# Experts' loop of a two-block transformer on one core: all twelve low parts of a block's weights on VectorE

## The reference, cut to what matters

```python
for e in range(N_EXPERTS):
    he = jax.nn.silu(h @ w1[e]) * (h @ w3[e])
    out = out + gates[:, e:e + 1] * (he @ w2[e])
```

## Time and profile before

| what | value |
|---|---|
| median of three runs | 2589.7 us |
| the profiled execution | 2601.98 us, of which the span from first to last instruction is 2600.2 us |
| experts' loop in the trace | about 2243 to 2574 us of the span |
| one turn, from the third on | 18.50 us |
| TensorE busy over the span | 2328.2 us (90%) |
| VectorE busy over the span | 1598.8 us (61%) |
| GpSimd busy over the span | 177.3 us (7%) |
| mean granted TensorE clock | 0.941 of full speed |

### The profile page before, as it was taken

How to read it: one execution, slowest core, us unless ns; L and a number is a source line. 1 busy time by engine, 2 the same in 40 slices (tenths; PEclk the granted TensorE clock), 3 DMA queues, 4 the chain that set the end, 5 groups by cost and what they waited for, 6 DMA issues and landing times. The chain is left out here.

```text
span 2600.2 us, 32144 instructions
## 1 busy us (share of the span) xinstructions
PE 2328.2 (90%) x11490; PEld 1867.7 (72%) x11490; DVE 1598.8 (61%) x2267; ACT 1067.3 (41%) x1615; POOL 177.3 (7%) x201
## 2 busy tenths in 40 slices
PE   4998688899999999878979999999997788799995
PEld 3777566678878777757757888788885676577774
DVE  6564656555566555465655555763353765599996
ACT  3443234333351334233344333323313434577774
POOL 0001100000000000101000000000000001122222
PEclk9998899899999899789889999998996999799997
DMA  7640000222235355000012222442365001699995
GB/s 295 221 158 1 1 34 1 81 87 90 97 118 189 104 191 182 20 1 2 33 49 81 97 89 95 165 156 89 107 218 193 1 1 42 267 397 397 396 397 211
DMA packets 95239, 348.20 MB, mean 134 GB/s; under 512 B 12288, under 2 KB 14352, under 8 KB 94864
## 3 DMA queue, kind: packets, MB, share of 16 engines
q1 hardware_dynamic: 88496, 323.57, 35.3%
q0 software_dynamic: 3888, 14.16, 1.4%
q10 hardware_dynamic: 2736, 8.92, 0.8%
HBM read 333.50 MB, written 21.50 MB: 137 GB/s over the span
## 5 line engine op out<-in xcount | busy, mean ns | idle before, releaser
L498 PE MATMUL ps<-a_hi,w_hi 128*128 128x512 f32 x1408 | 571.5, 406 | 42.3 <-DVE y_lo L1775 19.3
L500 PE MATMUL ps<-a_hi,w_lo 128*128 128x512 f32 x1408 | 563.8, 400 | 0.0
L499 PE MATMUL ps<-h_lo,w_hi 128*128 128x512 f32 x1280 | 507.3, 396 | 0.0
L462 DVE TENSOR_TENSOR w_lo<-ring,w_hi 128x1024 fp32r<-128x1024 f32 x178 | 218.1, 1226 | 378.9 <-ACT w_hi L457 378.5
L457 ACT ACTIVATE w_hi<-ring 128x1024 fp32r<-128x1024 f32 x178 | 188.3, 1058 | 534.2 <-PE ps L500 521.0
L498 PEld LDWEIGHTS ps<-a_hi,w_hi 128*128 128x128 f32 x1408 | 268.2, 190 | 114.9 <-DVE w_lo L462 28.5
L500 PEld LDWEIGHTS ps<-a_hi,w_lo 128*128 128x128 f32 x1408 | 267.7, 190 | 66.3
L499 PEld LDWEIGHTS ps<-h_lo,w_hi 128*128 128x128 f32 x1280 | 243.2, 190 | 60.7 <-issue 2.9
L3061 DVE TENSOR_TENSOR moe_w_lo<-p,moe_w_hi 128x1024 fp32r<-128x1024 f32 x187 | 247.0, 1365 | 14.9 <-ACT moe_w_hi L3160 13.6
L3160 ACT ACTIVATE moe_w_hi<-p 128x1024 fp32r<-128x1024 f32 x204 | 216.1, 1062 | 68.8 <-PE ps L3103 61.3
L1998 PE MATMUL ps<-p_lo,down_hi 128*128 128x512 f32 x352 | 137.9, 392 | 0.0
(11 more groups left out here) (619 smaller groups left out, 4295.2 us busy)
## 6 DMA issues: line engine op xcount, KB each, us to landing
ring<-in_ffn_up SPq DMA_DIRECT2D x88, 512.0 KB, 3.4
ring<-in_w_in SPq DMA_DIRECT2D x72, 512.0 KB, 4.6
p<-in_moe_gate SPq DMA_DIRECT2D x68, 512.0 KB, 6.1
p<-in_moe_up SPq DMA_DIRECT2D x68, 512.0 KB, 5.5
p<-in_moe_down SPq DMA_DIRECT2D x68, 512.0 KB, 6.9
vt<-in_ada SPq DMA_DIRECT2D x64, 512.0 KB, 3.9
down_raw<-in_ffn_down SPq DMA_DIRECT2D x32, 704.0 KB, 4.9
y<-in_ada SPq DMA_DIRECT2D x32, 512.0 KB, 3.6
```

What stands on the lines that cost most here:

```text
L462: self.c.nc.vector.tensor_tensor(self.c.w_lo[:, s % 2, :], self.c.slot(s), self.c.w_hi[:, s % 2, :].bitcast(F32), ALU.subtract).then_inc(s ...
L498: nc.tensor.matmul(bank, c.w_hi[:, s % 2, at], hi(kt), start=(kt == 0), stop=False)
L499: nc.tensor.matmul(bank, c.w_hi[:, s % 2, at], lo(kt), start=False, stop=False)
L500: return nc.tensor.matmul(bank, c.w_lo[:, s % 2, at], hi(kt), start=False, stop=(kt == KT - 1))
```

## The change

VectorE makes the low part of chunk 5 too, between those of chunks 4 and 6. GpSimd's subtraction is replaced by an addition of one number per partition (zero plus zero into a spare column), which waits for nothing. Nothing else is touched: loads, ScalarE, TensorE and the semaphores stay, and `low[5]` is now set by VectorE.

```diff
+        self.spare = c.small.bitcast(I32)[:, 56:57]
...
             def body(j):
-                subtract_chunk(pool, nc.gpsimd, 5, j)
+                nc.gpsimd.tensor_tensor(m.spare, m.zero[:, 0:1], m.zero[:, 0:1], ALU.add)
                 choose(j + 2)
                 pool.wait_ge(now, j + 3)
                 nc.gpsimd.tensor_tensor(m.now[:, 1:2], m.zero[:, 0:1], m.zero[:, 0:1], ALU.add)
...
                 if not first(j):
                     lower_he(j - 1)
-                lower(j, (4, 6, 7))
+                lower(j, (4, 5, 6, 7))
                 if not first(j):
                     lower(j - 1, (8, 9, 10, 11))
                 product(j)
```

## The result

The changed kernel takes 2578.3 us in the median of five runs (2575.2 to 2583.2), the kernel before, timed with it, 2590.4. The ratio is 0.9939, interval 0.9920 to 0.9958: 15.8 us by the ratio, 12.1 by the medians, 12.9 by the means of the five and five. The kernel got faster, by about 12 us where 9.6 were forecast.

The account below looks back on a forecast made before the run. It took GpSimd's subtraction, which stalls TensorE and excludes VectorE, to bound the loop. Saving 14 by 0.63, 8.8 us, plus 0.8 at the end, 9.6 us, took 2589.7 to 2580.1 us; range 2577.5 to 2585.5.

Parts of the forecast that it names:

- TensorE's wait for GpSimd: In the loop, TensorE stalls 15 times on chunk 5's low part from GpSimd; 0.63 us a turn would come back.
- VectorE's full turn: In the loop, VectorE's old turn of 18.50 us included 1.59 standing still; it would lose 2.03 and gain 1.17.
- The turn: One loop turn, set by TensorE, would fall from 18.50 to 17.87 us.
- 14 stalls: Stalls of turns 2 to 15 removed, 14 by 0.63 us: 8.8 us saved.
- VectorE's sum: VectorE's new loop turn from pitches, twelve low parts by 1.17 plus other work: 17.64 us, 0.23 under TensorE's.
- The second rival: In the loop, GpSimd's small operations hold VectorE up, up to 0.19 us each; time 2585.3 us; chance 0.08.
- The end: After the loop, VectorE reaches the last block's chunk 10 low part about 0.8 us earlier: 0.8 us saved.
- VectorE's share: At the end, VectorE's earlier arrival at the low part of chunk 10, about 0.8 us.
- Transfers: First rival: in the loop, transfers take over as the bound; 2581 to 2585 us, say 2583; chance 0.12.
- New stall on VectorE: In the loop, TensorE waits for VectorE at chunk 4 or 5; gain gone, about 2589 us; chance 0.07.
- The stretch not GpSimd's: In the loop, VectorE's long low part has another cause and its 1.59 us stay; 2600.7 us; chance 0.04.

Follow-up runs that it names:

- Experiments 3: Changed kernel, but GpSimd subtracts unrelated tiles at its old moment, for nobody, in place of the small addition; ratio 1.0048 to the kernel before, turn 19.54 us.
- Experiment 4: Changed kernel, but GpSimd makes the low part of the previous block's chunk 10, in time, VectorE the other eleven; ratio 0.9989 to the kernel before, turns 18.37 us.
- Experiment 6: Changed kernel plus a GpSimd fill of 128 x 3072 unused numbers with zeros, reading nothing; ratio 0.9965 to the kernel before, turns 17.83 us.
- experiment 5: Changed kernel with VectorE's low parts in order 4, 6, 5, 7, so chunk 5's is late; ratio 1.0050 to the kernel before, turns 18.96 us.
- the other two old ones: Second and third traces of the kernel before, unchanged; from first transposes of gathered rows to the end 359.0 and 359.7 us.
- the repeats: The changed kernel, unedited, timed twice more against the kernel before; ratio 0.9952 both times.
- experiment 2: Changed kernel without GpSimd's small addition; ratio 0.9959 to the kernel before, turns 17.83 us.

## Why the prediction was right in its way and too small

**What bounded the kernel.** Right: VectorE and GpSimd exclude each other. Experiments 3 and 4 show it, with low parts of 3.42 and 2.16 us where 1.21 is the rule. Experiment 6 shows that a GpSimd fill of 2.67 us doesn't do it; that this is because a fill doesn't read SBUF is likely, but no run isolates it. I gave TensorE's wait for GpSimd the leading part and VectorE's full turn a second one. Experiment 4 shows that the freeze alone suffices: with the wait gone and the freeze left, 0.13 of 0.67 us return. And the wait itself came of the exclusion: GpSimd started at 2397.61 and takes 2.41 us alone, so it would have been done at 2400.02, ahead of TensorE's 2400.35 (an estimate from the rows and sums of the prediction).

**The turn.** Forecast 17.87, measured 17.83, with 0.67 us back where the sum had 0.63. Over 14 stalls that is 9.3 and not 8.8 us (from the first transposes to those of turn 15: 295.25 us in the first old trace, 285.96 in the new). The 36 matmuls of the second turn, which I took for TensorE's free pace, still had a little of the rising clock in them: 8.25 us, or 8.21 as I corrected them, where the changed kernel takes 8.17.

**VectorE's sum** was wrong, and by luck on the safe side. The four low parts that gave 1.17 us each have 0.14 us of idle time before the last; back to back one costs 1.135. VectorE's own turn is 17.21 us and not 17.64, its idle time in the changed kernel 0.62 and not 0.23, and the stretch in the old kernel 1.73 (2.948 less 1.216) and not 1.59. The second rival would have needed 0.62 us a turn, not 0.23. The hand-overs came as worked out: chunk 4's low part is ready 0.46 us before TensorE wants it (forecast 0.4), chunk 5's 0.68 (forecast 0.65). An order worse by one subtraction costs 1.13 us a turn (experiment 5).

**The end: the step that was mis-sized.** This term is the step of the sum that failed, more than the 0.5 us of the stalls. The sum had 0.8 us beyond the 14 stalls. Measured were 2.5 between the first two traces, 1.3 to 1.6 against the other two old ones, and 1.9 on the average of three and three (from the transposes of turn 15 to the end: 65.6, 64.4 and 64.4 us before, 63.1, 62.9 and 62.8 after). VectorE's share came out as forecast: the low part of the last block but one's chunk 10 ended 17.12 us earlier in absolute time, of which 7.01 lay ahead of the loop and 9.29 were stalls, which leaves 0.82. "The load, output and final sums follow unchanged" was the wrong sentence: it put at nothing, without a reason, the change in the load's landing. The load after it landed in 5.16, 4.93 and 4.96 us in the traces of the changed kernel (6.08, 5.63 and 5.80 before), 0.8 us sooner on average, as much again as VectorE's share. Why it lands sooner I did not test. Between the first two traces TensorE's last 24 matmuls also took 7.5 and not 8.7 us, since fewer of them ran at the half clock (7 and 12 matmuls of 0.63 us); the other two old traces have 7.5 and 7.4, so this part is chance of the first.

**The time.** Stalls 9.3 and end 1.3 to 2.5 make 10.6 to 11.8 us; the three and three loops differ by 11.0, the three ratios say 12.4 twice and 15.8 once. The forecast of 9.6 was 13 to 23% under these 11.0 to 12.4. On the old median of 2589.7 the repeats give 2577.3, just under the range's 2577.5, and the first ratio 2573.9. So of the 6.2 us between 9.6 and that first 15.8, 0.5 are the stalls and 0.5 to 1.7 the end. The other 4 or 5 lie in no turn and at no end that the traces show, and their cause stays open. Chance is enough to explain them: loop starts scatter by 18 us whichever kernel runs (2225.5 to 2243.0 in the eleven traces of the changed kernel and its variants), and the same five and five runs give 12.1 us by their medians. That the change moves something ahead of the loop is not excluded by three old traces. The range had been drawn for the loop's unknowns and left out this scatter of everything ahead of it; that was its fault.

**The rivals.** *Transfers:* not seen in the time, and nearer than I thought. I judged 397 GB/s not to be the most and was right; the most in this loop is 411 to 412, just what TensorE's turn asks for. At 2% less, by the same arithmetic, the first rival would have eaten into the gain. *Small operations:* nothing (experiment 2). *New stall on VectorE:* none in the turns; TensorE is busy throughout. *The stretch not GpSimd's:* refuted, none of 204 is above 1.227 us.

## What to carry to other kernels

Work given to GpSimd that reads SBUF need not be free for VectorE: here a subtraction of 2.4 us cost VectorE 0.95 to 2.2 us of standing still (low parts of 2.16, 2.95 and 3.42 us) to spare it 1.135. Where it falls counts as much as its length: the 0.95 us fell in a chain with 0.46 to spare and cost 0.54 a turn. When two engines disturb each other and a third waits, test lateness and freezing apart (an unneeded operation at the same place; the same operation where it is in time) before crediting either. Take an engine's own pace from a stretch without any pause: 0.14 us of idle time hidden in four operations made VectorE's floor 0.43 us too high. And ask of every floor under the one that is removed how far down it lies: here TensorE's 17.83 us and the transfers' 17.8 were the same.

## What the runs showed of the hardware that was not expected

A DMA share near 1 said little: it was 1.02 at 397 GB/s with loads landing after 5.9 to 6.7 us, 1.03 at 412 with 7.8 to 8.1, and 1.03 at 411 with 15.8. The landing times told when the transfers had become the bound; the share and the rate did not.

The loop starts between 2226.4 and 2244.3 us after the same code, and between the two traces at the ends of that range it went with the clock. These are the stretches 0:500, 500:1060 and 1060:1400 us of the kernel before in its second trace (loop start 2244.3) and in its third (2226.4), columns as above, the granted clock third from the end:

```profile
0.00:500.00 500.00, 409.13 (x2277) 323.66 (x2278) 295.74 (x532) 185.83 (x366) 25.21 (x46) 0.91 0.28 99
500.00:1060.00 560.00, 540.88 (x2288) 429.63 (x2287) 331.71 (x379) 210.31 (x272) 3.79 (x5) 0.98 0.38 129
1060.00:1400.00 340.00, 288.48 (x1727) 230.03 (x1726) 191.95 (x415) 121.53 (x274) 21.77 (x38) 0.86 0.07 22
```

```profile
0.00:500.00 500.00, 411.80 (x2284) 322.67 (x2285) 295.63 (x532) 185.97 (x366) 25.38 (x46) 0.95 0.28 100
500.00:1060.00 560.00, 540.98 (x2290) 429.07 (x2288) 331.78 (x379) 212.70 (x276) 4.75 (x6) 0.98 0.38 128
1060.00:1400.00 340.00, 284.17 (x1790) 226.76 (x1789) 200.60 (x426) 125.95 (x278) 20.49 (x36) 0.93 0.08 27
```

Between 500 and 1060 us both had 0.98. In the two stretches beside it, where TensorE is busy for a smaller share (409 of 500 and 288 of 340 us, against 541 of 560), the execution with the later loop start had the lower mean clock, 0.91 against 0.95 and 0.86 against 0.93. What decides that from one execution to the next I did not test.
